# Prompt scores beside the sample's search: narrower units, three buffers, rounds under the loads, later folds

## What is computed

```python
def dsa_attend(q, qi, wi, q_pos, ki_all, topk, gather_kv, rel_bias):
    dots = jnp.einsum('bthd,bsd->bths', qi, ki_all) * (D_IDX ** -0.5)     # 8 index heads of 64
    score = jnp.einsum('bth,bths->bts', wi, jax.nn.relu(dots)).astype(jnp.float32)
    causal = jnp.arange(L)[None, :] <= q_pos[:, None]
    score = jnp.where(causal[None], score, -jnp.inf)
    vals, sel = lax.top_k(score, topk)                                    # topk = 256
    ...                                                                   # gather, bias, softmax, values
```

## Time and profile before

| | us |
|---|---|
| runs shown | 4769.36, 4774.19, 4771.5 |
| median | 4771.5 |
| the profiled execution | 4774.26 |
| its span, first to last instruction | 4772.7 |
| the stage of the change, first load issued to last mask | 1276.2 to 1632.9 |

### The profile page before, as it was taken

One profiled execution on the slowest core, in us unless ns is written; L12 is line 12 of the kernel. 1 busy time (PEld: TensorE's weight loads), 2 busy tenths in 40 slices (PEclk: granted clock), 3 DMA queues, 4 the chain that ended last, 5 costly groups with the idle time before them and its releaser, 6 DMA issues. The chain is left out here.

```text
span 4772.7 us, 53427 instructions
## 1 busy us (share of the span) xinstructions
PE 4033.1 (85%) x19170; PEld 3186.5 (67%) x19170; DVE 2863.0 (60%) x4793; ACT 2014.4 (42%) x3045; POOL 374.8 (8%) x315
## 2 busy tenths in 40 slices
PE   8999987677767558874399977999999999999998
PEld 7888876664445324543288866878778787877884
DVE  5678646994368788888578864434544453454320
ACT  3333324552257559885377652133223312322310
POOL 0000003443211011110010000000000000000000
PEclk9999977888867779996599988999999999999967
DMA  5555553223301034422311123323342342334345
GB/s 162 158 170 151 149 141 93 70 75 85 100 27 31 1 122 169 151 100 80 103 47 36 29 73 102 97 84 97 103 123 94 101 132 85 96 90 131 97 136 183
DMA packets 481958, 486.33 MB, mean 102 GB/s; under 512 B 96152, under 2 KB 396152, under 8 KB 473144
## 3 DMA queue, kind: packets, MB, share of 16 engines
q1 hardware_dynamic: 457336, 364.66, 26.4%
q0 software_dynamic: 23104, 118.50, 7.0%
q10 hardware_dynamic: 1280, 0.02, 0.0%
HBM read 422.20 MB, written 60.90 MB: 101 GB/s over the span
## 5 line engine op out<-in xcount | busy, mean ns | idle before, releaser
L2441 ACT ACTIVATE weight_parts<-weights 128x1024 fp32r<-128x1024 f32 x296 | 313.4, 1060 | 1194.0 <-PE acc L2768 561.0
L2768 PE MATMUL acc<-act_T,weight_parts 128*128 128x512 f32 x3072 | 705.8, 392 | 17.9 <-DVE act_T L2563 17.9
L2792 PE MATMUL acc<-weight_parts,hidden_parts 128*128 128x512 f32 x3072 | 702.3, 391 | 9.0 <-DVE product_rows L2570 9.0
L2556 DVE TENSOR_TENSOR weight_parts<-weights,weight_parts 128x1024 fp32r<-128x1024 f32 x296 | 363.1, 1228 | 570.5 <-ACT weight_parts L2441 567.3
L2768 PEld LDWEIGHTS acc<-act_T,weight_parts 128*128 128x128 f32 x3072 | 582.4, 190 | 140.6 <-issue 12.0
L2792 PEld LDWEIGHTS acc<-weight_parts,hidden_parts 128*128 128x128 f32 x3072 | 579.8, 189 | 131.5 <-issue 6.1
L532 PE MATMUL accumulated<-hT,w_in_parts 128*128 128x512 f32 (+1 forms) x1920 | 431.3, 391 | 5.4 <-DVE w_in_parts L385 5.4
L532 PEld LDWEIGHTS accumulated<-hT,w_in_parts 128*128 128x128 f32 x1920 | 368.0, 215 | 66.9 <-DVE w_in_parts L385 7.4
L2651 DVE TENSOR_SCALAR hidden_T<-acc 128x512 f32<-128x512 f32 (+1 forms) x160 | 95.7, 598 | 445.4 <-PE acc L2768 356.0
L306 ACT ACTIVATE w_in_parts<-w_in_raw 128x1024 fp32r<-128x1024 f32 (+1 forms) x140 | 141.9, 1015 | 462.0 <-PE accumulated L532 264.0
L2136 ACT ACTIVATE junk_act<-score,candidate 128x1920 bf16<-128x1920 f32 (+6 forms) x224 | 292.5, 1314 | 90.8 <-DVEq L2202 69.8
(11 more groups left out here) (347 smaller groups left out, 6710.4 us busy)
## 6 DMA issues: line engine op xcount, KB each, us to landing
weights<-in_w_up SPq DMA_DIRECT2D x160, 512.0 KB, 4.0
weights<-in_w_down SPq DMA_DIRECT2D x160, 512.0 KB, 3.6
w_in_raw<-in_w_in SPq DMA_DIRECT2D x100, 512.0 KB, 4.0
weights<-in_w_out SPq DMA_DIRECT2D x40, 512.0 KB, 3.6
w_in_raw<-in_w_in SPq DMA_DIRECT2D x60, 256.0 KB, 3.4
x_sb<-in_x_prompt POOLq DMA_DIRECT2D x4, 2048.0 KB, 9.9
q_rows<-scratch_qT SPq DMA_DIRECT2D x64, 128.0 KB, 3.6
mix_in<-scratch_mix POOLq DMA_DIRECT2D x4, 2048.0 KB, 9.3
```

Of the source, the lines that this page charges most:

```text
L2441: act.activation(w2[:, w, 0, :], raw[:, b[0], :], ACT.Copy).then_inc(hi_rdy, 1)
L2556: dve.tensor_tensor(w2[:, w, 1, :], raw[:, b, :], w2[:, w, 0, :].bitcast(F32), ALU.subtract).then_inc(lo_rdy, 1)
L2768: mm = pe.matmul(acc[:, u % 8, 0:w], w2[:, u % 2, b, k * P:(k + 1) * P], aT[:, a, k, 0:w], start=(k == 0 and (a, b) == (0, 0)), stop=(k == ...
L2792: mm = pe.matmul(acc[0:pt, 2 * t + half, :], hs[:, d % 2, a, t * pt:(t + 1) * pt], w2[:, d % 2, b, half * ST:(half + 1) * ST], start=(d == ...
```

## The change

The limit under which a tile is one unit goes from 1536 to 1024 columns, so tiles 8 to 11 are split as well: 176 units. `dots` and `R` get three buffers of 1024 columns instead of two of 1536, and the waits go one unit further back. Three rounds of the search run before the first unit: two before the keys are split, one after it. The other 29 are spread over the units (0, 9, 17, 24, 30, 36, 41, ... 171), at least four units apart. The update stands ahead of unit u+3 and the fold on TensorE ahead of the dots of unit u+5; the last round's fold stands behind all units. SP loads the search's constants first, then the keys, the first queries and the rest.

```diff
-    UNITS = [... if WIDTH[i] <= 3 * ST else [(0, 2 * ST), (2 * ST, WIDTH[i] - 2 * ST)])
+    UNITS = [... if WIDTH[i] <= 2 * ST else [(0, 2 * ST), (2 * ST, WIDTH[i] - 2 * ST)])
-        R = sb("relu", [P, 2, 3 * ST])
+        RB, DB = 3, 3
+        R = sb("relu", [P, RB, 2 * ST])
-        dots = ps("dots", [P, 2, 3 * ST])
+        dots = ps("dots", [P, DB, 2 * ST])
-        ROUNDS = 32
+        ROUNDS, EARLY, FOLD, UPDATE = 32, 3, 5, 3
+        count_at = {r: int(np.searchsorted(units_wide, units_wide[-1] * (r - EARLY) // (ROUNDS - EARLY), "right")) - 1
+                    for r in range(EARLY, ROUNDS)}
+        for r in range(EARLY + 1, ROUNDS):
+            count_at[r] = max(count_at[r], count_at[r - 1] + UPDATE + 1)
+        LATE_FOLD = [r for r, u in count_at.items() if u + FOLD >= len(UNITS)]
+        LATE_UPDATE = [r for r, u in count_at.items() if u + UPDATE >= len(UNITS)]
 SP:
+                for dst, n in ((biti, "bits"), (bitn, "bits_negated"), (fold, "fold"), (fold2, "fold_twice")):
+                    sp.dma_start(dst[:, :], io[n]).then_inc(search_rdy, 16)
                 sp.dma_start(kiT[:, :], sc["kiT"][:, 0:T]).then_inc(ki_rdy, 16)
+                load_q(0)
                 sp.dma_start(wi[:, :, :], ...
 TensorE:
                 pe.wait_ge(search_rdy, 64)
+                for r in range(EARLY):
+                    fold_counts(r)
                 pe.wait_ge(k_lo, 1)
                 for u, (i, c0, wide, h) in enumerate(UNITS):
...
-                    if u >= 2:
-                        pe.wait_ge(relu_done, u - 1)
+                    if u >= DB:
+                        pe.wait_ge(relu_done, u - DB + 1)
+                    if u - FOLD in round_of:
+                        fold_counts(round_of[u - FOLD])
...
-                    if u - 2 in round_of:
-                        fold_counts(round_of[u - 2])
...
+                for r in LATE_FOLD:
+                    fold_counts(r)
 ScalarE:
+                for r in range(EARLY - 1):
+                    count(r)
                 act.wait_ge(ki_rdy, 16)
                 act.activation(kh[:, :], kiT[:, :], ACT.Copy).then_inc(k_hi, 1)
                 q_high(0)
+                count(EARLY - 1)
...
-                    if u >= 2:
-                        act.wait_ge(acc_done, u - 1)
+                    if u >= RB:
+                        act.wait_ge(acc_done, u - RB + 1)
 VectorE:
+                dve.wait_ge(search_rdy, 64)
+                link(dve.memset(cand_s[:, :], 0))
+                link(dve.memset(ncand_s[:, :], 0))
+                dve.sem_inc(cand_rdy, 1)
+                for r in range(EARLY - 1):
+                    count(r)
+                    update(r)
                 dve.memset(sent[:, :], SENT).then_inc(z_rdy, 1)
                 dve.wait_ge(z_rdy, 1)
                 dve.wait_ge(k_hi, 1)
                 dve.tensor_tensor(kiT[:, :].bitcast(F32R), kiT[:, :], kh[:, :].bitcast(F32), ALU.subtract).then_inc(k_lo, 1)
+                count(EARLY - 1)
+                update(EARLY - 1)
...
-                    if u - 1 in round_of:
-                        update(round_of[u - 1])
+                    if u - UPDATE in round_of:
+                        update(round_of[u - UPDATE])
```

More of the change, by code:

```diff
@@ L875, in score_prompt_and_search_sample @@
 def score_prompt_and_search_sample(nc, io, sc, score, score_s, keep):
-    UNITS = [(i, c, w, h) for i in SEARCHED for c, w in ([(0, WIDTH[i])] if WIDTH[i] <= 3 * ST else [(0, 2 * ST), (2 * ST, WIDTH[i] - 2 * ST)])
+    UNITS = [(i, c, w, h) for i in SEARCHED for c, w in ([(0, WIDTH[i])] if WIDTH[i] <= 2 * ST else [(0, 2 * ST), (2 * ST, WIDTH[i] - 2 * ST)])
              for h in range(IH)]
@@ L910, in score_prompt_and_search_sample @@
         search_rdy, cand_rdy, as_cnt, ds_cnt, folded, chain_s = (sem("i_s_" + n) for n in ("const", "cand", "act", "dve", "folded", "chain"))
-        ROUNDS = 32
+        ROUNDS, EARLY, FOLD, UPDATE = 32, 3, 5, 3
         units_wide = np.cumsum([0] + [w + 250 for i, c, w, h in UNITS])
[L915 to L918, removed]
+        count_at = {r: int(np.searchsorted(units_wide, units_wide[-1] * (r - EARLY) // (ROUNDS - EARLY), "right")) - 1
+                    for r in range(EARLY, ROUNDS)}
+        for r in range(EARLY + 1, ROUNDS):
+            count_at[r] = max(count_at[r], count_at[r - 1] + UPDATE + 1)
+        assert count_at[ROUNDS - 1] < len(UNITS)
+        round_of = {u: r for r, u in count_at.items()}
+        LATE_FOLD = [r for r, u in count_at.items() if u + FOLD >= len(UNITS)]
+        LATE_UPDATE = [r for r, u in count_at.items() if u + UPDATE >= len(UNITS)]
         with nc.Block() as block:
@@ L922, in _, with load_q @@
             def _(sp):
[L923 to L934, removed]
+                def load_q(n):
+                    i, b = SEARCHED[n], n % 2
                     for half in range(2):
@@ L938, in _ @@
                             sp.dma_start(qr[r:r + 64, b, half:IH:2, :], src).then_inc(q_rdy[b], 16)
+                for dst, n in ((biti, "bits"), (bitn, "bits_negated"), (fold, "fold"), (fold2, "fold_twice")):
+                    sp.dma_start(dst[:, :], io[n]).then_inc(search_rdy, 16)
+                sp.dma_start(kiT[:, :], sc["kiT"][:, 0:T]).then_inc(ki_rdy, 16)
+                load_q(0)
+                sp.dma_start(wi[:, :, :], sc["wi"][0:T, :].rearrange("(i p) h -> p i h", p=P)).then_inc(const_rdy, 16)
+                sp.dma_start(later[:, :], io["later"]).then_inc(const_rdy, 16)
+                sp.dma_start(rb[:, :], io["rel_bias"]).then_inc(b_const, 16)
+                sp.dma_start(rb31[:, :], io["rel_bias"][BUCKETS - 1:BUCKETS, :].to_broadcast([BUCKETS, HEADS])).then_inc(b_const, 16)
+                sp.dma_start(boh[:, :], io["bucket_of"]).then_inc(b_const, 16)
+                for n in range(1, NSRCH):
+                    if n >= 2:
+                        sp.wait_ge(q_lo, n - 1)
+                    load_q(n)
                 sp.wait_ge(bt_rdy, HEADS)
@@ L970, in _ @@
                         k = slice(c0 + c, c0 + c + w)
-                        pe.matmul(dots[:, u % 2, c:c + w], qs[:, b, h, :], kh[:, k], start=True, stop=False)
-                        mm = pe.matmul(dots[:, u % 2, c:c + w], qs[:, b, h, :], kiT[:, k].bitcast(F32R), start=False, stop=True)
+                        pe.matmul(dots[:, u % DB, c:c + w], qs[:, b, h, :], kh[:, k], start=True, stop=False)
+                        mm = pe.matmul(dots[:, u % DB, c:c + w], qs[:, b, h, :], kiT[:, k].bitcast(F32R), start=False, stop=True)
                     mm.then_inc(dots_done, 1)
-                    if u - 2 in round_of:
-                        fold_counts(round_of[u - 2])
                     if u in head_at:
@@ L987, in q_high, with count @@
                     act.activation(qs[:, n % 2, :, :], qr[:, n % 2, :, :], ACT.Copy).then_inc(q_hi, 1)
+                def count(r):
+                    act.wait_ge(cand_rdy, r + 1)
+                    act.wait_ge(as_cnt, r)
+                    act.activation(ja_s[:, :], score_s[:, ND_S:NEWC], ACT.Sign, bias=ncf_s[:, 0:1], accum_out=ca[:, 0:1])\
+                        .then_inc(as_cnt, 1)
+                for r in range(EARLY - 1):
+                    count(r)
                 act.wait_ge(ki_rdy, 16)
@@ L994, in _ @@
                     act.wait_ge(dots_done, u + 1)
-                    if u >= 2:
-                        act.wait_ge(acc_done, u - 1)
-                    act.activation(R[:, u % 2, 0:wide], dots[:, u % 2, 0:wide], ACT.Relu).then_inc(relu_done, 1)
+                    if u >= RB:
+                        act.wait_ge(acc_done, u - RB + 1)
+                    act.activation(R[:, u % RB, 0:wide], dots[:, u % DB, 0:wide], ACT.Relu).then_inc(relu_done, 1)
                     if u in round_of:
[L999 to L1003, removed]
+                        count(round_of[u])
             @block.vector
@@ L1059, in _ @@
                         dve.tensor_copy(skew[:, head_at[u - 1], :], bt).then_inc(bt_rdy, 1)
+                for r in LATE_UPDATE:
+                    update(r)
                 dve.wait_ge(z_rdy, 1 + NSRCH)
```

6 lines of the change are left out of this document (1 added, 5 removed).

## The result

The changed kernel takes 4741.9 us (median of 4 runs, 4738.6 to 4746.7) beside 4770.7 of the kernel before: a ratio of 0.9939, 95% interval 0.9922 to 0.9956, so 29 us faster (21 to 37). The forecast was 4754.5, within 4740 to 4768: the right side, but 17 us of gain where about 29 came.

What follows compares the result with a forecast made beforehand. No engine is full: VectorE waits each search round on the loop of ScalarE's count, TensorE's fold and its own update. Tiles 5 to 15 give -19.9, start and early units +3.1: -17 us from 4771.5, 4754.5 (4740 to 4768).

Steps and rivals of the forecast that it cites:

- VectorE would set the length of tiles 5 to 15, and its fold waits would go: Tiles 5 to 15: without its waits VectorE sets the pace; 274.3 us become 254.4, 19.9 less.
- Waits left: Tiles 5 to 15: VectorE waiting that remains uncovered after the change, put at 4 us (0 to 12).
- wait for relus not above 8: Sign in the profile after: VectorE's wait for ScalarE's relus stays at or below 8 us.
- the 32 extra units: Splitting tiles 8 to 11: 0.34 us of VectorE per added unit, 10.9 us in all (7.4 to 10.9).
- ScalarE leads, so the third buffer covers: Tiles 5 to 15: ScalarE may lead by three units, covering its count by 1 us; the fold barely at low clock.
- The start: Before the first dots: early counts and subtractions delay them to about 1295.8 us, 3.2 us later (bounds 1 and 6).
- Units 0 to 23: Before tile 5: the eight bias matmuls bind; unit 24 3 us late in all (5 earlier to 6 later).
- the fold's new wait: Units 0 to 23: each fold adds some 3.3 us, about what two rounds in the bias chain cost now.
- still about 4.8: Sign in the profile after: the bias matmuls remain about 4.8 us apart.
- TensorE as the bound (1): From unit 24 on: TensorE at low clock leaves some 15 us of waiting, -6 us, 4765; chance 17%.
- The slower case (2): Fold behind two more units' dots: VectorE waits 1.6 us in each of 26 rounds, +21, 4792; chance 8%.
- The better case (3): Early stretch gains too, by TensorE's high clock or third buffer and one round less: -12 more, 4742; chance 8%.

Runs made afterwards that it cites:

- e4: Kernel before (two buffers of 1536 columns, 144 units, no early rounds) with only the later fold and update, second count after unit 9: 4770.1 us, 0.9998 of before.
- e7: Changed kernel with two buffers of 1024 columns for `dots` and `R` instead of three: 4798.3 us, 1.0057 of before.
- e8: Changed kernel with the fold ahead of the dots of unit u+3 instead of u+5: 4761.7 us, 0.9980 of before.
- e3: Changed kernel without early rounds, fold ahead of dots u+2 (one unit earlier than before), update ahead of unit u+1: 4792.2 us, 1.0046 of before.
- e6: Changed kernel with the eight bias matmuls moved to units 52, 60, ... 108 from 6, 8, ... 20: 4729.1 us, 0.9916 of before.
- e12: Kernel before with only the bias matmuls moved, to units 50, 58, ... 106: 4757.3 us, 0.9971 of before.

## Why the prediction was right, and where it was not

**VectorE would set the length of tiles 5 to 15, and its fold waits would go: right.** 31.0 us became 2.8 and 1.1. The stretch fell from 274.5 (mean of three) to 254.0 (of two), 20.5 us; forecast 19.9. Inside, terms moved against each other. Waits left: of the 36.5 us of both waits before, 6.5 were to stay and 4 to come; 19.7 and 16.6 were there, so 13.2 and 10.1 came, about my bound of 12. That is the mis-sized term (the count and the queries' copy in one gap, and the narrow units; my sign "wait for relus not above 8" failed with 15.4). Against that, the 32 extra units cost 8.0 us of VectorE's busy time (its multiplies and adds 165.7 us for 157.7) where 10.9 had been charged with gaps, and the GpSimd collisions fell: `F_s<-F_s,kept_bit_s` took 6.0 us of 26 for 13.1 of 28, its neighbour `candidate_s` 6.4 for 4.5. So the waiting term was too small, and that the sum still came within 1 us is luck: the other terms erred the other way. The sum also has a pace for the whole stretch and doesn't say where the gain falls, all of it outside the tiles that are split.

**ScalarE leads, so the third buffer covers: right, but only with the fold's place.** The prediction named the dots of unit u+5 as what is queued behind the fold, but priced the fold's place only as a risk. e4, e7 and e8 show that it is half of the mechanism: with the third buffer and the fold at its old place tiles 5 to 15 gain nothing (e8), with the fold one unit earlier still they lose 23 us (e3), a later fold without a buffer gives nothing (e4) or harm (e7), both together give the gain.

**The start: right.** First dots were forecast 3.2 us later; they came 2.5 later (19.9 for 17.4). The rows, SP's queue among them, against the earlier trace rows:

```profile
1265.54 0.33 SPq L935 DMA_DIRECT2D bits<-in_bits  x1
...
1269.15 2.96 ACT L1003 ACTIVATE junk_act_s<-scoreS,minus_candidate_s 128x3200 bf16<-128x3200 f32 x1 [13.30 <-DVEq L1048]
...
1277.29 1.89 ACT L1009 ACTIVATE ki_high<-kiT 128x2048 fp32r<-128x2048 f32 x1
...
1279.82 2.29 DVE L1055 TENSOR_TENSOR kiT<-kiT,ki_high 128x2048 fp32r<-128x2048 f32 x1
...
1280.21 4.11 POOL L956 TENSOR_TENSOR qi_parts<-qi_rows,qi_parts 64x1024 fp32r<-64x1024 f32 x1 [32.40 <-DMA qi_rows<-scratch_qiT]
...
1284.47 0.66 PE L983 MATMUL dots<-ki_high,qi_parts 128*128 128x384 f32 x1 [0.16 <-POOL qi_parts L956]
```

The GpSimd subtraction takes 4.11 us where it takes 2.36 elsewhere, since VectorE's subtraction holds it up. By the rule of the Trainium skill that the prediction weighed ("SBUF — State Buffer", section "Who interferes with whom"), the two exclude each other for a whole instruction; the trace agrees, with 1.75 us. But that cost the start nothing: the subtraction ends at 1284.32 and the third fold, which also stands ahead of the first dots, at 1284.30. The prediction would have taken 1.7 us off its sum without this rule, and that was wrong.

**Units 0 to 23: wrong, by 7 us.** The step "walking it unit by unit I reach unit 24 3 us late" failed: it came 4 us early (79.6 for 83.4). It had the bound right: e6 and e12 take the bias matmuls out and win 21 us of this stretch each. What it had wrong is the price of a round in this chain. It put the fold's new wait, 3.3 us, level with what two rounds cost before. A pair without a round takes 4.8 us, and in the kernel before the pair with the round counted after unit 8 takes 8.75, so one round alone cost 3.95. That pair starts with this bias matmul and ends with the one at 1317.66:

```profile
1308.91 1.61 PE L979 MATMUL bias_turned<-bucket_of,rel_bias_wide 32*128 32x384 f32 x2 [1.27 <-DVE minus_bias L1059]
```

In the changed kernel the bias matmuls stand 5.88, 5.87, 6.81, 5.12, 6.44 and 6.00 us apart from the second on (my sign "still about 4.8" failed). The round counted after unit 9, with its late fold, costs 4.2 in the first three of these, and the pair with the fold 2.0 of them where I had 3.3. So a round is no dearer than before, and there is one less. Tiles 2, 3 and 4 take 12.1, 23.7 and 22.0 us for 14.5, 29.7 and 20.3: the gain is in tile 3, where two rounds were counted and now one is, and in tile 2, which no run took apart. The 4 us are within the bound of 5.

**Rivals.** TensorE as the bound (1) did not come: its granted clock is 0.80 for 0.79 in the long stretch and it waits for relus. The Trainium skill's rule ("TensorE: Matmul & The Clock Gate", "A second HAM failure mode: psum-queue depth-cycling") would have the clock swing and bring 4765; it does swing (0.80 is a mean of the two levels), but as before, and the run gives 4742. The slower case (2) did not come with the change, but e7 comes nearest to it: 32.4 us of fold waits and 44.0 of relu waits, 4798. There, with two buffers of 1024 columns, ScalarE's lead no longer covers its count. The better case (3) named the early stretch and a total of 4742, and 4742 came, but by luck: the early stretch gave 7 of its 12 us, TensorE stayed at the low clock there (0.50 in the profile), and most of the rest is the part outside the stage.

**What stays open**: the 4 to 8 us between the medians' gain and the stage's. Of the 12.6 us between forecast and median, 7 lie ahead of tile 5 (start and units 0 to 23), 1 in tiles 5 to 15, and the rest there.

## What to carry to other kernels

When an engine runs its work in order, a wait in its queue holds up all that stands behind it. A buffer more is then never filled if the producer waits ahead of the slot that it adds. Here the fold ahead of dots u+3 left the third buffer empty, and ahead of dots u+5 it did not (u+4 was not tried). Ask of each buffer change which waits of the producer's queue come ahead of the new slot, and judge it with that wait moved; each half alone can measure as useless or harmful. And when a small side job (here eight bias tiles) sits in a stretch that waits in a circle, move it to one where its engines run ahead: it gave 10 to 13 us more for one line.

## What the runs showed that was not expected

A wait can vanish from the row where it is looked for and cost as much elsewhere: with the fold at u+3 VectorE's wait for the folded counts is 0.2 us, and the kernel is 20 to 23 us slower than with it at u+5, through 76 us of TensorE standing at the fold. Stages whose code was the same in all the profiles ended up to 12 us apart (1263.7 to 1275.3), so that one profile against one profile can't place a change of this size by its absolute times; lengths of the stage itself repeat within 2 to 3 us.
